# A bidirectional state-space scan: two masked exponentials become one behind a predicated copy, and the order of the work around it changes

## The reference, cut to what matters

```python
def segsum_exp(a):
    cs = jnp.cumsum(a, axis=-1)
    diff = cs[..., :, None] - cs[..., None, :]
    L = a.shape[-1]
    mask = jnp.tril(jnp.ones((L, L), dtype=bool))
    return jnp.exp(jnp.where(mask, diff, -jnp.inf))
...
    decay = segsum_exp(a_dt)
    cb = jnp.einsum('bclgn,bcsgn->bcgls', c, b)
    y_diag = jnp.einsum('bcgls,bcgrls,bcsgrp->bclgrp', cb, decay, xdt)
...
    y_fwd = ssd_scan(xs, dt[:, :, 0], a[0], bs, cs)
    fl = lambda t: jnp.flip(t, axis=1)
    y_bwd = fl(ssd_scan(fl(xs), fl(dt[:, :, 1]), a[1], fl(bs), fl(cs)))
    y = y_fwd + y_bwd + xs * d_skip.astype(jnp.float32).reshape(G, R, 1)
    y = gated_rmsnorm(y.reshape(Bsz, S, D_INNER), z, norm_w)
```

## Time and profile before

| | |
|---|---|
| median of 3 runs | 942.24 us (942.22 to 942.31) |
| the profiled execution's own time | 942.23 us |
| its span, first to last instruction | 940.4 us |
| TensorE's granted clock | 1.00 throughout |
| busy share: TensorE, VectorE, ScalarE, GpSimd | 99%, 70%, 54%, 6% |

### The profile page before, as it was taken

One profiled execution on the slowest core, in us unless ns is written; L12 is line 12 of the kernel. 1 busy time (PEld: TensorE's weight loads), 2 busy tenths in 40 slices (PEclk: granted clock), 3 DMA queues, 4 the chain that ended last, 5 costly groups with the idle time before them and its releaser, 6 DMA issues.

```text
span 940.4 us, 13246 instructions
## 1 busy us (share of the span) xinstructions
PE 932.4 (99%) x5362; PEld 807.9 (86%) x5362; DVE 662.4 (70%) x946; ACT 507.6 (54%) x664; POOL 60.8 (6%) x68
## 2 busy tenths in 40 slices
PE   9999999999999999999999999999999999999998
PEld 8988899988888888888888888899888898888887
DVE  6779789998878764778776446767665758776433
ACT  6457876676555733456554335755653455554331
POOL 1000000023321000000003310000000000000000
PEclk9999999999999999999999999999999999999999
DMA  8943233554224475435447955353355435546551
GB/s 306 341 168 124 93 133 135 180 167 169 91 90 157 140 307 197 169 131 221 179 180 236 256 196 206 136 205 128 123 217 179 179 135 217 187 179 224 178 179 45
DMA packets 25278, 166.51 MB, mean 177 GB/s; under 512 B 2987, under 2 KB 3115, under 8 KB 6657
## 3 DMA queue, kind: packets, MB, share of 16 engines
q1 hardware_dynamic: 22464, 156.12, 46.1%
q0 software_dynamic: 2752, 9.54, 3.5%
HBM read 164.57 MB, written 1.08 MB: 176 GB/s over the span
## 4 chain that ended last, share of the span: by engine, by line
PE 86%; DVE 11%; ACT 2%; issue 1%; ACTq 0%; DVEq 0%
PE ps L393 54%; PE ps L582 11%; PE ps L587 6%; DVE conv_acc L1688 5%; DVE w_lo L1455 3%; PE ps L843 1%; PE ps L772 1%; PE ps L787 1%; PE ps L424 1%; PE ps L426 1%; PE ps L433 1%; PE ps L512 1%; PE ps L630 1%; PE ps L893 1%; PE ps L852 1%
## 5 line engine op out<-in xcount | busy, mean ns | idle before, releaser
L1455 DVE TENSOR_TENSOR w_lo<-raw,w_hi 128x2048 fp32r<-128x2048 f32 x145 | 331.3, 2291 | 181.0 <-ACT w_hi L1075 180.8
L1075 ACT ACTIVATE w_hi<-raw 128x2048 fp32r<-128x2048 f32 x145 | 275.5, 1906 | 179.1 <-PE ps L393 160.2
L393 PE MATMUL ps<-w_hi,ht 128*128 128x512 f32 (+1 forms) x576 | 181.4, 388 | 0.0
L393 PE MATMUL ps<-ht,w_hi 128*128 128x256 f32 (+1 forms) x816 | 150.6, 286 | 0.0
L393 PEld LDWEIGHTS ps<-ht,w_hi 128*128 128x128 f32 (+1 forms) x816 | 126.2, 190 | 4.1 <-issue 4.0
L393 PEld LDWEIGHTS ps<-w_hi,ht 128*128 128x128 f32 x576 | 107.3, 188 | 22.4 <-issue 1.1
L393 PE MATMUL ps<-ht,w_lo 128*128 128x256 f32 (+1 forms) x408 | 115.3, 282 | 0.0
L393 PE MATMUL ps<-w_lo,ht 128*128 128x512 f32 (+1 forms) x288 | 110.5, 384 | 0.0
L582 PE MATMUL ps<-ht,w_hi 128*128 128x512 f32 x448 | 109.5, 391 | 0.0
L393 PE MATMUL ps<-w_hi,ff_hi 128*128 128x512 f32 x256 | 99.7, 389 | 0.0
L393 PE MATMUL ps<-w_lo,ff_hi 128*128 128x512 f32 x256 | 99.6, 389 | 0.0
(11 more groups left out here) (301 smaller groups left out, 1217.4 us busy)
## 6 DMA issues: line engine op xcount, KB each, us to landing
raw<-in_w_stream SPq DMA_DIRECT2D x145, 1024.0 KB, 4.8
bias<-rel_scratch POOLq DMA_DIRECT2D x1, 3072.0 KB, 21.2
bias<-in_rpb POOLq DMA_DIRECT2D x16, 128.0 KB, 7.9
x_first<-in_x_in SPq DMA_DIRECT2D x2, 512.0 KB, 4.1
raw<-in_w_stream SPq DMA_DIRECT2D x2, 512.0 KB, 6.4
gates<-in_gate_bias POOLq DMA_DIRECT2D x4, 256.0 KB, 6.0
gates<-in_gate_bias POOLq DMA_DIRECT2D x2, 512.0 KB, 7.2
x<-in_x_in POOLq DMA_DIRECT2D x1, 1024.0 KB, 5.3
```

Of the source, the lines that this page charges most:

```text
L393: ins = pe.matmul(o, still, moving, start=first and n == 0, stop=last and n == 2, skip_group_check=True)
L1075: act.activation(split_home(s)[0][:, 0:width(s)], raw[s % RAW_RING][:, 0:width(s)], ACT.Copy).then_inc(hi_ready, 1)
L1455: dve.tensor_tensor(lo[:, 0:width(s)], raw[s % RAW_RING][:, 0:width(s)], hi[:, 0:width(s)].bitcast(F32), ALU.subtract).then_inc(lo_ready, 1)
```

## The change

Each group's two masked exponentials become one. TensorE makes the two unmasked differences in banks 5 and 6 (no `far`, no `unit`). VectorE copies the backward ones over the forward ones in PSUM where the table `tri[:, 2]` is not zero, by a predicated copy (`ssd_choose`). ScalarE takes one exponential of bank 5. The diagonal's second term, which now has no place in the table, is C·B of each token with itself times the backward step size: VectorE multiplies B and C (`make_twins`), TensorE sums the products by 16 matmuls with one column (`twin_sums`), and VectorE adds the result to `d_skip` (`own_terms`). ScalarE instead of GpSimd makes `cum_s` from the second group on. The silu of the second half of z is taken at once in slot 31. VectorE's order in slots 28 to 36 is written out anew in `scan_slot`, and there it splits piece s+1 in slot s instead of s+2; in slot 28 it splits none, in slots 37 and 38 piece s+1, in slot 39 pieces 40 and 41.

```diff
@@ -857,15 +858,22 @@
-                if g == 0 and c == 0:
-                    pe.wait_ge(far_ready, 1)
                 for d in range(2):
                     key = ("decay", g, c, d)
                     claim(key, 5 + d)
                     pe.matmul(ps[:, 5 + d, :], cum_s[g % 2][:, 2 * c + d, :], cum_l[c][:, d, :, :],
-                              start=True, stop=False)
-                    pe.matmul(ps[:, 5 + d, :], unit[:, :], far[:, d].unsqueeze(1).to_broadcast([P, PER_GROUP, P]),
-                              start=False, stop=True).then_inc(*fill_of(key))
+                              start=True, stop=True).then_inc(*fill_of(key))
+            def twin_sums():
+                claim("twins", 4)
+                pe.wait_ge(twins_ready, 4)
+                for c in range(RT):
+                    for g in range(GROUPS):
+                        at0 = c * GROUPS + g
+                        ins = pe.matmul(ps[:, 4, at0:at0 + 1], twins[2 * c + g // 4][:, g % 4, :], tri[:, 0, P - 1:P],
+                                        start=True, stop=True)
+                ins.then_inc(*fill_of("twins"))
             def cumulate():
@@ -904,6 +912,8 @@
+                    if s == 29:
+                        twin_sums()
@@ -1147,15 +1157,12 @@
-                for d, dest in enumerate((decay[g % 2][c], decay_back[c])):
-                    key = ("decay", g, c, d)
-                    ready(act, key)
-                    if d == 0 and g >= 2:
-                        ready(act, ("y", g - 2))
-                    if d == 1 and g:
-                        act.wait_ge(decay_scaled, 2 * g - 1 + c)
-                    act.activation(dest[:, :, :], ps[:, 5 + d, :].rearrange("p (h l) -> p h l", h=PER_GROUP),
-                                   ACT.Exp).then_inc(*drain_of(key))
+                key = ("decay", g, c, 0)
+                emptied(act, ("decay", g, c, 1))
+                if g >= 2:
+                    ready(act, ("y", g - 2))
+                act.activation(decay[g % 2][c][:, :, :], ps[:, 5, :].rearrange("p (h l) -> p h l", h=PER_GROUP),
+                               ACT.Exp).then_inc(*drain_of(key))
@@ -1307,6 +1314,26 @@
+                if 0 <= s - 29 < GROUPS:
+                    key = ("state", s - 29)
+                    ready(act, key)
+                    act.activation(state[:, :, :], ps[:, 7, :].rearrange("p (a b) -> p a b", a=2),
+                                   ACT.Copy).then_inc(*drain_of(key))
+                if 0 <= s - 28 < GROUPS:
+                    decay_exps(s - 28, 1)
+                if 0 <= s - 28 < GROUPS - 1:
+                    g = s - 27
+                    if g == 1:
+                        act.wait_ge(cum_s_ready, 1)
+                    else:
+                        ready(act, ("decay", g - 2, 1, 1))
+                    act.activation(cum_s[g % 2][:, :, :], cum[:, :, :], ACT.Identity, scale=quad[:, 10 + g:11 + g],
+                                   bias=quad[:, 18 + g:19 + g]).then_inc(cum_s_ready, 1)
+                if s == 31:
+                    for c in (2, 3):
+                        emptied(act, ("z", c, 0)), emptied(act, ("z", c, 1))
+                    act.activation(zg_half[1][:, :, :], zg_half[1][:, :, :], ACT.Silu).then_inc(z_last_silu, 1)
+                    act.preload_act_table(ACT.Exp)
...
+                if s == 27:
+                    act.preload_act_table(ACT.Exp)
                 if name == "z" and closes:
+                    if chunk == 3:
+                        ready(act, "twins")
                     for r in range(RT):
                         key = ("z", chunk, r)
                         ready(act, key)
                         act.activation(zg(r, chunk * 512, 512), ps[:, bank(key), :],
-                                       ACT.Silu if chunk else ACT.Copy).then_inc(*drain_of(key))
+                                       ACT.Silu if chunk == 1 else ACT.Copy).then_inc(*drain_of(key))
                 if s == 26:
@@ -1699,40 +1723,99 @@
+            def ssd_choose(g, c):
+                ready(dve, ("decay", g, c, 0)), ready(dve, ("decay", g, c, 1))
+                both = [ps[:, 5 + d, :].rearrange("p (h l) -> p h l", h=PER_GROUP) for d in range(2)]
+                dve.copy_predicated(both[0], tri[:, 2].bitcast(I32).unsqueeze(1).to_broadcast([P, PER_GROUP, P]),
+                                    both[1]).then_inc(*drain_of(("decay", g, c, 1)))
             def ssd_weigh(g, c):
-                emptied(dve, ("decay", g, c, 0)), emptied(dve, ("decay", g, c, 1))
-                w = decay[g % 2][c]
-                link(dve.tensor_tensor(w[:, :, :], w[:, :, :], decay_back[c][:, :, :], ALU.add))
+                emptied(dve, ("decay", g, c, 0))
                 if c == 0:
                     emptied(dve, ("cb", g))
+                w = decay[g % 2][c]
                 dve.tensor_tensor(w[:, :, :], w[:, :, :],
                                   cb[:, c, :].unsqueeze(1).to_broadcast([P, PER_GROUP, P]),
                                   ALU.mult).then_inc(decay_scaled, 1)
+            def make_twins():
+                dve.wait_ge(conv_silu, 8)
+                for c in range(RT):
+                    for half in range(2):
+                        first, tokens = 4 * half, slice(c * P, c * P + P)
+                        dve.tensor_tensor(twins[2 * c + half][:, :, :], bc[:, first:first + 4, tokens],
+                                          bc[:, GROUPS + first:GROUPS + first + 4, tokens],
+                                          ALU.mult).then_inc(twins_ready, 1)
+            def scan_slot(s):
+                g, last = s - 28, s - 29
+                if g < GROUPS:
+                    ssd_choose(g, 0)
+                    ssd_weigh(g, 0)
+                if last > 0:
+                    ssd_skip(last)
+                if g < GROUPS:
+                    ssd_choose(g, 1)
+                if last == 0:
+                    own_terms()
+                    ssd_skip(0)
+                if g == 0:
+                    make_twins()
+                else:
+                    split_lo(s + 1)
+                if g < GROUPS:
+                    ssd_weigh(g, 1)
+                if s == S_GATE + 5:
+                    dve.wait_ge(gate_bias_second, 32)
+                    gate_bias(1)
+                if last >= 0:
+                    ssd_gate(last)
+            def own_terms():
+                ready(dve, "twins")
+                v = own_skip[:, :, :].rearrange("p c (g h) -> p c g h", g=GROUPS)
+                for c in range(RT):
+                    ins = dve.tensor_tensor(v[:, c], dt[:, c, HEADS:2 * HEADS].rearrange("p (g h) -> p g h", g=GROUPS),
+                                            ps[:, 4, c * GROUPS:c * GROUPS + GROUPS].unsqueeze(2)
+                                            .to_broadcast([P, GROUPS, PER_GROUP]), ALU.mult)
+                ins.then_inc(*drain_of("twins"))
+                emptied(dve, "twins")
+                link(dve.tensor_tensor(own_skip[:, :, :], own_skip[:, :, :],
+                                       param("d_skip").unsqueeze(1).to_broadcast([P, RT, HEADS]), ALU.add))
+            def ssd_skip(g):
+                for c in range(RT):
+                    ins = dve.tensor_tensor(skipped[:, c, :].rearrange("p (h d) -> p h d", h=PER_GROUP),
+                                            xtok(c, g * GW, GW).rearrange("p (h d) -> p h d", h=PER_GROUP), per_head(own_skip[:, c, 4 * g:4 * g + 4], 4), ALU.mult)
+                link(ins)
             def ssd_gate(g):
                 own = xtok(all_rows, g * GW, GW)
                 ready(dve, ("y", g))
-                dve.wait_ge(x_state_ready, 2 * (g + 1))
-                for c in range(RT):
-                    v = xtok(c, g * GW, GW).rearrange("p (h d) -> p h d", h=PER_GROUP)
-                    ins = dve.tensor_tensor(v, v, per_head(param("d_skip")[:, 4 * g:4 * g + 4], 4), ALU.mult)
-                link(ins)
                 ready(dve, ("off", g))
                 for i in range(RT):
                     ins = dve.tensor_tensor(y_off[:, i].rearrange("p (h d) -> p h d", h=PER_GROUP),
                                             ps[:, 7, i * GW:i * GW + GW].rearrange("p (h d) -> p h d", h=PER_GROUP),
                                             per_head(sums[:, i, 4 * g:4 * g + 4], 4), ALU.mult)
                 ins.then_inc(*drain_of(("off", g)))
-                dve.tensor_tensor(own, ps[:, 4, :].rearrange("p (c f) -> p c f", c=2), own, ALU.add).then_inc(*drain_of(("y", g)))
+                dve.wait_ge(x_state_ready, 2 * (g + 1))
+                dve.tensor_tensor(own, ps[:, 4, :].rearrange("p (c f) -> p c f", c=2), skipped[:, :, :], ALU.add).then_inc(*drain_of(("y", g)))
                 emptied(dve, ("off", g))
                 emptied(dve, ("y", g))
                 link(dve.tensor_tensor(own, own, y_off[:, :, :], ALU.add))
                 if g == 0:
                     dve.wait_ge(z_first_silu, 1)
@@ -1818,8 +1901,8 @@
```

(19 more changed lines are left out.)

35 lines of the change are left out of this document (10 added, 25 removed).

## The result

The changed kernel took 947.94 us (median of 7 runs, 945.52 to 952.13), the kernel before 942.24 beside it: ratio 1.006, 95% interval 1.0045 to 1.0075. That is slower by 0.6%, outside my range of 941.0 to 946.0, and 4.4 us above the 943.5. The profiled execution is the shortest of the seven: 945.52 us, span 943.7.

A forecast was written before the change was run, and what follows sets the result against it. TensorE was taken to bound the kernel, VectorE close behind. From 942.23: −7.4 (`far`) −0.4 (old wait) +3.5 (twin sums) +1.1 (slot 28) +4.5 (slot 40) = +1.3, giving 943.5 us, range 941.0 to 946.0.

The forecast's parts named there:

- `far` gives back 0.9 us a slot: TensorE scan slots: dropping 32 mask matmuls at 0.23 us saves 7.4 us, 0.92 in each slot with four.
- the old wait: TensorE's only scan wait, 0.38 us in front of `cb` of group 2, was to go: −0.4 us.
- the twin sums take 3.5: TensorE in slot 29: 16 one-column matmuls, 32 records at 0.108 us, add 3.5 us.
- slot 28 waits 1.0 for 1.1: TensorE in slot 28 waits 1.1 us for ScalarE's exponential, behind VectorE's late first predicated copy.
- the split of piece 40: VectorE splits piece 40 behind four `yt_lo`, so TensorE waits 4.5 us at the head of slot 40.
- my cover for piece 39: Piece 39 ready at 311.9, wanted by TensorE at 311.92: just hidden; 0.1 to 0.3 us more if that fails.
- Rivals 1 to 4: No slot 40 wait: 939.0, 6%; copy 1.37 us: 945.7, 14%; twins near free: 940.0, 4%; slot 31 ScalarE late: 945.4, 3%.
- the fifth: VectorE falls behind by its own waits, so slots 29 to 34 lose 1 to 2 us: 945; 8%.
- the first part: What bounds the kernel: TensorE in slots 29 to 38 and beyond, with no later idle stretch to swallow a wait.
- the 7.4 us: The whole saving on TensorE from removing the 32 `far` matmuls at 0.23 us from start to start.

The follow-up runs named there:

- those of the second: The changed kernel timed once more, unchanged, against the kernel before: 951.2 us (948.14 to 952.73), ratio 1.0088.

## Why the prediction was wrong

**What held.** `far` gives back 0.9 us a slot, the old wait goes, the twin sums take 3.5, slot 28 waits 1.0 for 1.1, the split of piece 40 comes too late and TensorE waits 4.5 in two parts (my cover for piece 39 failed by 0.41, more than the 0.1 to 0.3 I allowed, and slot 40 waited 0.4 less). The profiled execution of the first measurement is 2.0 above the sum of these terms, 1.6 of it at half clock. Rivals 1 to 4 are out: the slot 40 wait is there, the copy takes 0.69, the twins cost their weight loads, and ScalarE's table load in slot 31 delays no slot, since the slot after it starts on time, 10.4 us behind. So is the fifth: the steady slots last 10.4.

**The step that failed** is in the first part: "A microsecond that it does not issue is gained, and a microsecond that it waits is lost". It isn't one for one. My sum has no term for the clock at which TensorE runs behind a wait and behind the twin sums; it put that at nothing without a reason. In the median execution, with a clock of 0.995, this term is 4.7 us by the estimate above, against the 4.4 by which the sum was short.

- The wait. In the kernel before, 3.3 us of it cost 5.2 in the median and 3.5 in the one execution of five that kept its clock; with the wait filled the clock there stays at 1.00. In the changed kernel, 4.1 us brought 1.6 more in one profile, and the stretch was 6.8 us long in another.
- The twin sums. I priced them by their weight loads, "3.5 us, all of it on TensorE's path". In the kernel before such a run costs 7.6, and the same run with 128 columns 3.1, which leaves 4.5 for the half clock. In the changed kernel with piece 40 early fifteen of the sixteen cost 7.3 to 7.8, between the medians 945.0 and 937.7 or 937.2. I compared one column with 32 columns for the distance of starts alone, and that distance was right. What differed was the clock behind them.

The clock behind a wait could have been in my sum. The Trainium skill, page "TensorE: Matmul & The Clock Gate", section "HAM oscillation — how this bites in real kernels", tells of a kernel whose TensorE waits for transfers and goes on at half rate after every wait, and it counts half of the throttled time as lost. The rows agree on the wait: by that page the 3.41 us at half clock cost an estimated 1.7, and the count of matmuls gave 1.6. For the 10.24 us behind the twins the page's half would be an estimated 5.1, the medians gave 4.0 to 4.5; where the rest went stays open. That kernel's TensorE waited; here it lost its clock at the twin sums without a wait.

With those in, the sum is 943.5 + 4.5 (twins) + 1.6 (wait) = 949.6 where both triggers work, and 945.1 where only the wait does. The seven executions of the first measurement lie from 945.5 to 952.1, those of the second from 948.1 to 952.7. A profile exists of one execution in each, so where the others lost their clock is argued from the experiments. Why the same program has the stretch behind the twin sums in most executions and not in all, and why it is 6.8 us long in one and 10.2 in another, stays open.

I also took for granted that the 7.4 us would be had. They were (slots of 10.4), but not by the removal alone: in the kernel before without `far` only 4.1 came. The rest of the change brings the rest, by difference; I didn't try its parts (the order in `scan_slot`, the one exponential, `cum_s` on ScalarE) one by one.

## What to carry to other kernels

On a path where TensorE never rests, price a new wait or a new run of narrow matmuls twice: its own length, and the slower stretch behind it. The stretch doesn't come in every execution, so give it a range. Look at the granted clock of every stretch in which TensorE waits or has few columns, before summing. Sums over a diagonal that another engine can take from a table at hand are better taken there, if that engine has the time in its slot; and before calling it full, look for an idle gap that another piece of its own work can fill, and for work that would be shorter where GpSimd idles.
